# Memory-input projections in plain fp32, moved into the scores and into the gaps at the norms; bias and maximum in one instruction; values taken two heads at a time

## The reference, cut to what matters

```python
# block 1
h = rms_norm(x, g);  proj = h @ w_in                    # q, k/v of three kinds, gates, pool, u, v
out_a = nsa_mixer(...)      # 8 heads; compressed (15 columns), selected and window attention, with a bias
                            # softmax over s + bias; at 256 rows both kinds see all causal keys
x = x + rms_norm(concat(out_a, out_b, out_c) @ w_out, g)
m = rms_norm(mem, g)                                     # depends on mem alone
q = rms_norm(x, g) @ w_mq;  k = m @ w_mk;  v = m @ w_mv  # 1024 x 1024 each
x = x + rms_norm(softmax(q k^T / 16) v @ w_mo, g)
x = x + rms_norm(conv_ffn(rms_norm(x, g), w_up, ...), g) # 22 pairs of 256 columns up, 11 units down
# block 2
mem_n = rms_norm_2(mem_2, g)                             # depends on mem_2 alone
proj = rms_norm_2(x, g) @ w_in_2   # delta rule, top-k attention over 256 positions, 31-tap conv
x = x + concat(...) @ w_out_2
kv = mem_n @ xa_wkv                                      # keys 512 columns, values 512 columns
x = x + cross_attention(x, kv) @ xa_wo
x = x + relu(rms_norm_2(x, g) @ w1)**2 @ w2
```

## Time and profile before

| | us |
|---|---|
| three runs | 988.30, 994.08, 2722.09 |
| median of the runs | 994.08 |
| profiled execution, device time | 990.52 |
| span of the profiled execution, first to last instruction | 988.5 |
| TensorE busy | 922.9 (93%) |
| VectorE busy | 582.6 (59%) |
| ScalarE busy | 410.7 (42%) |
| POOL busy | 130.8 (13%) |

### The profile page before, as it was taken

One profiled execution on the slowest core, in us unless ns is written; L12 is line 12 of the kernel. 1 busy time (PEld: TensorE's weight loads), 2 busy tenths in 40 slices (PEclk: granted clock), 3 DMA queues, 4 the chain that ended last, 5 costly groups with the idle time before them and its releaser, 6 DMA issues.

```text
span 988.5 us, 13536 instructions
## 1 busy us (share of the span) xinstructions
PE 922.9 (93%) x5638; PEld 798.8 (81%) x5638; DVE 582.6 (59%) x784; ACT 410.7 (42%) x583; POOL 130.8 (13%) x174
## 2 busy tenths in 40 slices
PE   6998799899899999999989888989998889999998
PEld 5995697669769999999688887778667679999997
DVE  4338665452746877676568993664264547555552
ACT  4238342332534545444355534512153426444440
POOL 0140000020020000000129881240000000000000
PEclk9996799999999999999998989799999999999999
DMA  7962253306305755655045232100150418656631
GB/s 258 309 192 86 80 217 114 101 22 214 124 25 204 246 190 176 208 170 188 27 138 163 86 128 86 43 1 1 43 213 22 149 46 295 198 187 192 191 128 43
DMA packets 92344, 136.00 MB, mean 138 GB/s; under 512 B 4435, under 2 KB 76763, under 8 KB 92028
## 3 DMA queue, kind: packets, MB, share of 16 engines
q1 hardware_dynamic: 90428, 129.88, 39.9%
q0 software_dynamic: 736, 2.63, 0.8%
q10 hardware_dynamic: 1120, 2.62, 0.8%
HBM read 133.54 MB, written 1.06 MB: 136 GB/s over the span
## 4 chain that ended last, share of the span: by engine, by line
PE 80%; DVE 13%; issue 2%; ACT 2%; DMA 1%; POOL 1%; SPq 0%; POOLq 0%; DVEq 0%
PE work L1957 30%; PE acc L1957 25%; PE work L1938 7%; PE work L2397 3%; DVE hT L1312 2%; DVE split_operands L1327 1%; PE acc L2431 1%; DVE arena L1599 1%; ACT act_junk L878 1%; DVE split_extra_slot L1327 1%; PE work L2070 1%; PE work L2325 1%; PE work L2334 1%; PE acc L2167 1%; PE work L1944 1%
## 5 line engine op out<-in xcount | busy, mean ns | idle before, releaser
L1327 DVE TENSOR_TENSOR split_operands<-weight_ring,split_operands 128x2048 fp32r<-128x2048 f32 x72 | 165.8, 2305 | 89.4 <-ACT split_operands L898 88.8
L1957 PE MATMUL work<-split_operands 128*128 128x256 f32 x1680 | 208.0, 284 | 3.9 <-DVE split_operands L1327 3.9
L1957 PEld LDWEIGHTS work<-split_operands 128*128 128x128 f32 x1680 | 205.7, 193 | 6.1 <-issue 4.9
L1957 PE MATMUL acc<-split_operands 128*128 128x512 f32 x888 | 207.5, 390 | 0.1
L1957 PEld LDWEIGHTS acc<-split_operands 128*128 128x128 f32 x888 | 165.1, 188 | 33.8 <-DVE split_operands L1543 0.3
L898 ACT ACTIVATE split_operands<-weight_ring 128x2048 fp32r<-128x2048 f32 x72 | 137.4, 1911 | 103.8 <-PE acc L1957 49.3
L1957 PE MATMUL work<-split_operands,split_extra_slot 128*128 128x256 f32 x1152 | 145.5, 287 | 4.4 <-DVE split_extra_slot L1327 4.4
L1957 PEld LDWEIGHTS work<-split_operands,split_extra_slot 128*128 128x128 f32 x1152 | 142.8, 194 | 6.6 <-issue 5.8
L885 ACT ACTIVATE arena<-work 128x512 f32<-128x512 f32 (+1 forms) x69 | 38.6, 563 | 165.3 <-PE work L1957 81.8
L1327 DVE TENSOR_TENSOR split_extra_slot<-weight_ring,split_extra_slot 128x2048 fp32r<-128x2048 f32 x34 | 78.5, 2308 | 40.9 <-ACT split_extra_slot L898 40.4
L898 ACT ACTIVATE split_extra_slot<-weight_ring 128x2048 fp32r<-128x2048 f32 x34 | 64.9, 1910 | 48.0 <-PE work L1957 17.8
(11 more groups left out here) (291 smaller groups left out, 991.9 us busy)
## 6 DMA issues: line engine op xcount, KB each, us to landing
weight_ring<-in_mlp_w SPq DMA_DIRECT2D x32, 1024.0 KB, 5.7
weight_ring<-in_w_up SPq DMA_DIRECT2D x22, 1024.0 KB, 5.1
weight_ring<-in_w_in SPq DMA_DIRECT2D x20, 1024.0 KB, 6.1
weight_ring<-in_w_down SPq DMA_DIRECT2D x11, 1024.0 KB, 4.9
weight_ring<-in_w_out SPq DMA_DIRECT2D x8, 1024.0 KB, 4.9
weight_ring<-in_w_mk SPq DMA_DIRECT2D x4, 1024.0 KB, 6.2
weight_ring<-in_w_mv SPq DMA_DIRECT2D x4, 1024.0 KB, 6.0
weight_ring<-in_w_mq SPq DMA_DIRECT2D x4, 1024.0 KB, 5.4
```

Source lines behind the costliest of these rows:

```text
L1327: dve.tensor_tensor(slot[:, 1, :], weights(split_units[i], 2048), slot[:, 0, :], ALU.subtract).then_inc(low_ready, 1)
L1957: ins = pe.matmul(out, lhs(p), rhs(q), start=(start and n == 0), stop=(stop and n == 2))
```

## The change

1. `mk` and `mv` are no longer split: plain fp32 from the ring, with `memT` in place of `hT`; the norm `memkv` goes ahead of the compression. `mk` 0 and 1 are computed two steps a head behind the score matmuls, into two `acc` banks; `mv` follows the scores; `mk` 2 goes ahead of the transposes of the norm `mem`, `mk` 3 behind them.
2. The norm `mem2` and its copy in are moved from block 2 to the middle of the `mq` units. `xk` 0 and 1 stand ahead of and behind the transposes of the norm `ffn`, the values of `mem_2` ahead of and behind those of `mix2`, eight steps at a time. The dummies of the three norms are gone.
3. `mq` 0, `up` 0 and `ug0` are split, no longer plain; TensorE no longer waits for `hT` itself, but for its split parts.
4. Bias and maximum, here and in the top-k attention, are one `tensor_tensor_reduce` for each of the two parts.
5. `attend` takes two heads, whose outputs lie in the lower and upper 64 rows of one bank, matmul by matmul in turn; `probsT` has four buffers.
6. ScalarE's sums of squares write their unused output into `hT`; `xkT` has a tensor of its own.

```diff
-WHOLE = ("q0", ("mk", 0), ("mq", 0), ("up", 0), "ug0", ("xq", 0), ("m1", 0))
+WHOLE = ("q0", ("xq", 0), ("m1", 0))
-WARM_BEFORE = {"mem": 8, "ffn": 8, "mix2": 8, "cross": 2, "mlp": 2}
+WARM_BEFORE = {"cross": 2, "mlp": 2}
...
-    for product in ("mk", "mv", "out", "mq", "wo"):
-        units += [(product, c) for c in (MIX_ORDER if product == "out" else range(4))]
+    units += [("mk", 0), ("mk", 1)] + [("mv", c) for c in range(4)] + [("out", c) for c in MIX_ORDER]
+    units += [("mq", 0), ("mk", 2), ("mk", 3)] + [("mq", c) for c in range(1, 4)] + [("wo", c) for c in range(4)]
+    units += [("up", 0), ("xk", 0), ("xk", 1)]
...
-    units += ["ug0", "ug1", "cq", "ck", "ab"] + [("qkv", i) for i in range(6)] + [("z", 0), ("z", 1)]
-    units += [("xk", 0), ("xk", 1), ("xv", 0), ("xv", 1)] + [("out2", i) for i in MIX_ORDER]
+    units += ["ug0", ("xv", 0), ("xv", 1), "ug1", "cq", "ck", "ab"] + [("qkv", i) for i in range(6)] + [("z", 0), ("z", 1)]
+    units += [("out2", i) for i in MIX_ORDER]
...
-        phases = ((SPLIT_INPUTS, (None, 20480, 8704)), (("mk", "mv"), (None, 20480)),
+        phases = ((SPLIT_INPUTS, (None, 20480, 8704)),
                   (("out", "mq", "wo", "up", "down"), (None, 20480, 12288, 8192)),
                   (SPLIT_INPUTS_2 + ("qkv", "z"), (None, 20480)),
...
@@ ScalarE, at the end of the feed-forward @@
+            high_parts(upto("ug0"))
             post_squares("down", "down_post")
-            high_parts(upto("ug1"))
             next_squares("mix2", 4)
...
@@ VectorE, scores (the top-k attention likewise) @@
-                    dve.tensor_tensor(probs[t][h], bank(name)[:, 0:2 * n].rearrange("p (j s) -> p j s", j=2),
-                                      toeplitz[:, h, 0:n][:, ::-1].unsqueeze(1).broadcast_to([P, 2, n]), ALU.add
-                                      ).then_inc(reader(name), 1)
-                    dve.wait_ge(*drained(name))
-                    dve.tensor_reduce(soft[:, t, 0, h, 1:3], probs[t][h], AX, ALU.max, negate=True).then_inc(neg_max, 1)
-                low_parts(upto(("mk", 0)) + t)
+                    for j in range(2):
+                        ins = dve.tensor_tensor_reduce(probs[t][h][:, j, :], bank(name)[:, n * j:n * j + n],
+                                                       toeplitz[:, h, 0:n][:, ::-1], -1.0, LARGEST, ALU.add, ALU.min,
+                                                       soft[:, t, 0, h, j + 1:j + 2])
...
@@ TensorE @@
+            def mem_keys(out, name, source, steps):
+                w = weights(name, KD, 256)
+                for i in steps:
+                    c, k = i // KD, i % KD
+                    ins = pe.matmul(out[:, SEQ * c:SEQ * c + SEQ], w[:, k, P * c:P * c + P], source[:, k, :],
+                                    start=(k == 0), stop=(k == KD - 1))
+                return ins
...
                     pe.matmul(ps[:, 0:2 * n].rearrange("p (j s) -> p j s", j=2), qT[head_rows(h), h % HG, P * t:P * t + P],
                               keysT[head_rows(h), :, 0:n], start=True, stop=True).then_inc(tile_full, 1)
+                    i = HEAD_ORDER.index(h)
+                    if i == 0:
+                        pe.wait_ge(*loaded(("mk", t)))
+                    ins = mem_keys(acc(("mk", t)), ("mk", t), memT, (2 * i, 2 * i + 1))
...
-            norm_T("memkv", 2)
-            drained_norm("memkv")
-            pair_of_chunks(("mk", 0), ("mk", 0))
-            rows_split("memkv")
-            for c in range(1, 4):
-                split_pair(("mk", c), "memkv")
             open_product("mv")
             for i in range(4):
-                split_product_unit(("mv", i), i == 0, i == 3,
-                                   lambda p, kk, t: act_s["memkv"][p][:, 2 * i + kk, P * t:P * t + P])
+                pe.wait_ge(*loaded(("mv", i)))
+                for kk in range(2):
+                    for t in range(TT):
+                        for half in range(2):
+                            ins = pe.matmul(acc(("mv", 2 * t + half))[:, :], memT[:, 2 * i + kk, P * t:P * t + P],
+                                            weights(("mv", i), 2, D)[:, kk, 512 * half:512 * half + 512],
+                                            start=(i == 0 and kk == 0), stop=(i == 3 and kk == 1))
...
+            def attend(c):
...
+                for j in range(2):
+                    for i, h in enumerate(pair):
+                        pe.matmul(o[i], values[:, j, 0, vg], probsT[h % 4][:, j, 0, :], start=(j == 0), stop=False)
+                    for i, h in enumerate(pair):
+                        pe.matmul(o[i][:, P:SEQ], values[:, j, 1, vg], probsT[h % 4][:, j, 1, P:SEQ], start=False, stop=False)
...
             split_product("out", MIX_ORDER)
+            mem_keys_tile(("mk", 2), memT)
             norm_T("mem", 4)
-            drained_norm("mem")
-            pair_of_chunks(("mq", 0), ("mq", 0))
+            mem_keys_tile(("mk", 3), memT)
             rows_split("mem")
-            for c in range(1, 4):
+            for c in range(4):
+                if c == 3:
+                    norm_T("mem2", 6)
                 split_pair(("mq", c), "mem")
...
-            norm_T("ffn", 6)
-            drained_norm("ffn")
+            drained_norm("mem2")
+            mem_keys_tile(("xk", 0), mixT)
+            norm_T("ffn", 8)
+            mem_keys_tile(("xk", 1), mixT)
...
-            norm_T("mix2", 8)
-            drained_norm("mix2")
-            pair_of_chunks(("ug0",), "ug0")
+            cross_values(0)
+            norm_T("mix2", 10)
+            cross_values(1)
             rows_split("mix2")
+            split_pair(("ug0",), "mix2", "ug0")
...
-            norm_T("mem2", 10)
-            drained_norm("mem2")
-            pair_of_chunks(("xk", 0), ("xk", 0))
             row_sum("l")
...
-                cross_values(1)
```

More of the change, by code:

```diff
@@ L174, in plan @@
     norm("mix")
-    tiles.extend((n,) for n in ("q0", "q1", "bias_row", "kcvc", "kskw", "vsvw", "gates", "pool", "u", "v", "cmp_h", "cmp_kv"))
+    tiles.extend((n,) for n in ("q0", "q1", "bias_row", "kcvc", "kskw", "vsvw", "gates", "pool", "u", "v"))
+    norm("memkv")
+    tiles.extend((("cmp_h",), ("cmp_kv",)))
     for t in range(TT):
@@ L245, in plan @@
     fills = []
-    for product in ("mv", "o", "out", "wo", "down", "xv", "out2", "xwo", "m2"):
-        fills += [(product, i) for i in range(2 if product in ("o", "xv") else 4)]
+    for product in ("mk", "mv", "o", "out", "wo", "down", "out2", "xwo", "m2"):
+        fills += [(product, i) for i in range(2 if product in ("mk", "o") else 4)]
     return tiles, units, fills
@@ L505, in block_kernel @@
         vm = cut(18432, TT, D)
+        memT = cut(24576, KD, SEQ)
+        norm_target = {"memkv": memT, "mem2": mixT}
         hots = cut(16384, DIST_COLS)
@@ L623, in stat @@
             return stats[:, c:c + 1]
-        hT_free = {"mix": None, "memkv": full(("v",)), "mem": acc_filled(("mv", 3)), "ffn": full(("mq", 3))}
-        hT_free.update({"mix2": full(("up", FFN_PAIRS - 1)), "mem2": full(("z", 1)), "cross": acc_filled(("xv", 1)),
-                        "mlp": full(("xq", 1))})
+        hT_free = {"mix": None, "memkv": full(("v",)), "mem": full(("gates",)), "mem2": acc_filled(("out", 3)), "ffn": None,
+                   "mix2": None, "cross": full(("abw",)), "mlp": full(("xq", 1))}
         LAST_OF_UNIT = {u: full((u,)) for u in ("q0", "q1", "kcvc", "kskw", "vsvw", "gates", "pool", "u", "v")}
@@ L950, in _ @@
             ins.then_inc(reader(("cmp_h",)), 1)
[L952 to L955, removed]
             n = 0
@@ L1032, in _, with drain_cross_keys @@
             post_squares("wo", "wo_post")
-            high_parts(upto(("up", 2)))
             next_squares("ffn", 2)
+            def drain_cross_keys(c):
+                drain(("xk", c), xkT[:, 2 * c:2 * c + 2, :], halves(("xk", c))).then_inc(reader(("xk", c)), 1)
+            drain_cross_keys(0)
             high_rows("ffn")
+            drain_cross_keys(1)
             cw = parc("conv_w").rearrange("p (j g w) -> p j g w", g=2, w=3)
@@ L1493, in _ @@
             drain_norm("mem")
+            low_parts(upto(("mq", 3)))
+            drain_norm("mem2")
             low_parts(upto(("wo", 0)))
@@ L1552, in _ @@
                     gate_times_value(j - 1)
+            low_parts(upto("ug0"))
             post_norm("down", "down_post", 3)
@@ new lines, in attend @@
+                for i, h in enumerate(pair):
+                    r = slice(32 * (h % HG), 32 * (h % HG) + NCMP)
+                    ins = pe.matmul(o[i], cmp_v[r, vg], cmp_pT[r, g, :], start=False, stop=True)
+                return ins
+            for c in range(HEADS // 2 + 1):
+                if c < HEADS // 2:
+                    probs_T(2 * c)
+                    probs_T(2 * c + 1)
+                if c >= 1:
+                    attend(c - 1).then_inc(acc_full if (c - 1) % 2 == 1 else heads_done, 1)
```

230 lines of the change are left out of this document (121 added, 109 removed).

## The result

The changed kernel took **1023.0 us** (median of four runs, 1020.3 to 1024.0) against 995.7 for the kernel before; the ratio is 1.029, its 95% interval 1.026 to 1.033. It is slower; 985 us and a range of 969 to 1001 were forecast. The profiled execution took 1020.3 us.

What follows compares the result with a forecast made beforehand. TensorE was taken to bound the long runs of units, short steps of several engines the places between. Seven terms summed to -5.9 us on the profiled 990.5, giving 984.6, say 985 us; range 969 to 1001.

Steps and rivals of the forecast that it cites:

- A: First scores to the end of `mv`: key steps between scores, `mv` behind, ending at 147.3 us; -8.8 us, bounds -13.0 and -6.5.
- G: Delta rule: the value steps taken out had filled waits, only a few were in the way; -2.0 us, bounds 0 and -4.
- E: Norm `mix2`: values added, ScalarE waits for the down product, TensorE stands, clock falls; +8.8 us, bounds +6.4 and +11.
- F: Behind `z` 1: transposes and two `xk` units go, row sum starts earlier but cold; -8.5 us, bounds -12.5 and -5.
- B: `attend`: a pair of heads costs what one did, some given back; -6.0 us, bounds -8.1 and 0.
- C: Norm `mem` to the last `mq`: `mk` 3 and transposes added, split `mq` 0 and a wait saved; +6.4 us.
- D: Norm `ffn`: a unit added, a split unit and a wait saved, no third norm; +4.2 us.
- rival 2: Loads of `mq` 1, `up` 1 and `cq` each come a whole turn late, 31 us slower: 1016 us; chance 0.08.
- Rival 3: The fused instruction is slow: scores +13 us, top-k attention +4, giving 1002 us; chance 0.06.
- Rivals 1 and 4: First: no shape-change cost, full overlap, clock stays up, 971.9 us, chance 0.20. Second: A and B yield half, 992, chance 0.09.

Runs made afterwards that it cites:

- e1: The changed kernel with twelve dummies of 512 columns ahead of the first score matmul; 1005.2 us.
- e5: The kernel of e2_pairs with one dummy of 512 columns where each cross value step stood in the delta rule's chunks; 980.6 us.
- e3: The changed kernel with the score matmuls on all 128 rows instead of 64, so no change of shape against the key steps; 987.6 us, one run.
- e7: The kernel before with `attend` in pairs of heads and four buffers of probabilities, nothing else of the change; 989.6 us.
- e9_both: The kernel of e2_pairs with the dummies of e5 and the split slots from `ug0` on dealt out in the other order; 971.6 us.
- e10_more_dummies: The kernel of e9_both with dummies of 512 columns at five more places, 14 in all; 971.6 us.
- e2_pairs: The changed kernel with the score matmuls of two heads together, then four key steps; 986.1 us.
- e12_same_half: The kernel of e2_pairs with the heads reordered so that both of a pair use the same half of the rows; 994.0 us.

## Why the prediction was wrong

The step that failed is in A: "The first key work will meet a cold clock: `mk` 0 took 9.51 against 7.14 warm, so 2.4." That price belongs to an uninterrupted run of full-array matmuls, in which the clock came up within the first unit. The stage it was carried to changes between half-array and full-array matmuls 32 times, and there the clock did not come up at all. The rest of A was near, and on the safe side: the scores began at 79.4 for 81.2; a head at t = 1 was to take 0.89 + 0.89 + 0.26 = 2.04 and took 2.11 in e1; the stage warm was to take 34.4 and took 32.3; `mv` 27.7 for 27.5. Warm throughout, A would have ended near 142 (154.4 in e1, less the dummies' 12.2), not at 170.9. With the clock at half, 57 us of heads took the place of 29. A hint stood in the trace of before and was not used: its score matmuls ran at 0.50 from 80 to 91 us with TensorE busy throughout. I had asked of the clock only what a standstill does to it, never whether busy work brings it up.

G failed by the same omission seen from the other side. The step said that the value steps "filled waits" and so cost nothing; they did, and that filling kept the granted clock at 1.00 in the chunks, but for some 3 us. The prediction even followed the clock where dummies went (E and F), and not where real work that did the dummies' duty was taken away. Removing it cost 10.2 us there, by e5.

The drain at a change of shape, the rule of the Trainium skill that A weighed ("TensorEngine Tiling (Array Packing)", Key Properties), is in the rows of the runs: two key steps (four instructions) take 1.06 us between scores and 0.86 in e3 without a change, two score instructions 1.05 against 0.86. That is 0.39 a head, 0.20 for each change, where 0.13 was taken and 0.17 was the bound; over 32 changes some 2 us more than forecast. That a change has a price agrees with the rule; that the price is a drain and nothing else is not shown.

What was right: B (-7.2 for -6.0, all of it the pairing by e7), C and D (0.9 and 0.5 less than forecast; the loads of rival 2 were never late there, `mq` 1 follows `mq` 0 without a gap), E (the wait of ScalarE for the down product, TensorE standing 5.24 us, a clock of 0.50 behind it, and 5.5 us back when the slot is exchanged), F (-9.2 for -8.5), the levels of G, of the same length (6.44 us from one to the next in both). The terms written out for C and D add up to 6.3 and 4.1, not 6.4 and 4.2, which moves nothing. Rival 3, the slow fused instruction, was wrong in sign: it was worth 7 us to the kernel before, which the forecast had inside A without seeing it, as it compared with the measured 79.0 to 156.1. Rivals 1 and 4 named gains only. None of the rivals was a clock that stays low under load, and so the range stopped at 1001.

The last 3.3 us, behind the second mixer, were not explained by any edit. The cross scores and the first unit of the last stage, the same instructions as before, ran at a lower clock in this execution; the chain of the changed kernel, and below it of the kernel before:

```profile
832.19 8.52 PE work L1961 x32
```

```profile
803.78 7.14 PE work L1938 x32
```

e9_both has 7.14 there, e10_more_dummies 8.52 and e2_pairs 10.09, with the same code from the second output product on: it varies without any edit there, and what sets it is open. A part of the few us between medians and sums of stages is this.

## What to carry to other kernels

When work of another shape is laid between short matmuls, ask what clock the mixture gets, not only what the pieces cost: read the granted clock of the stretch as it is now, and group the pieces (two heads, four steps) so that the array changes its shape less often. When work that fills waits is moved away, ask what it did for the clock of what stands around it; dummies in its place restored 10.2 us here. And a slot, a buffer or a queue position that is dealt out by a rotation has to be dealt out anew for the changed list before any stage is priced.

## What the runs showed of the hardware

- TensorE without any idle time does not make the clock rise by itself. From the same low level, counted from the first score matmul, it rose after 6 us with full rows and no change of shape, 8 with pairs of heads in different halves, 12 with pairs in the same half, 13 with score matmuls alone (the kernel before), 25 with half rows and no change of shape; with a change of shape after every head it did not rise within the stage, and did 63 us after its start, at 142, when the stage was over. Started at the high level, that last mixture kept it. What exactly the chip counts stays open.
- Matmuls on different halves of the rows overlap: four instructions of 512 columns take 1.06 us (e2_pairs); on the same half they take 1.91, at the same clock, by this line of the chain of e12_same_half:

```profile
106.07 1.91 PE work L2151 x4
```

- The fused add and minimum on 256 columns starts again 0.35 us after the one before, its reading of the accumulator included (0.08), so 0.69 for a head's 512 columns, where an add and a reduction on 512 take 0.68 and 0.69.
